# A depthwise convolution shared between DVE and TensorE, in a fused three-layer fp32 kernel

## The reference

```python
def conformer_conv(x, w_pw1, b_pw1, w_dw, b_dw, g, b, w_pw2, b_pw2):
    h = x @ w_pw1 + b_pw1                       # 1024 -> 2048
    a, gate = jnp.split(h, 2, axis=-1)
    h = a * jax.nn.sigmoid(gate)
    h = lax.conv_general_dilated(               # depthwise, causal, 31 taps
        h, w_dw[:, None, :].astype(h.dtype), window_strides=(1,),
        padding=[(CONV_WIDTH - 1, 0)],
        dimension_numbers=("NWC", "WIO", "NWC"),
        feature_group_count=D_MODEL) + b_dw
    h = jax.nn.silu(layer_norm(h, g, b))
    return h @ w_pw2 + b_pw2
```

## Time and profile before

| what | value |
|---|---|
| median of 3 runs | 1508.88 us (1502.25 to 1509.17) |
| the profiled execution | 1508.11 us, span 1506.4 us |
| TensorE busy | 1368.4 us, 91% of the span |
| DVE, ScalarE, GpSimd busy | 373.2, 262.5, 24.3 us |
| chain that ended last | TensorE 88%, DVE 8%, DMA 2% |
| mean granted clock of TensorE | 0.94 |

### The profile page before, as it was taken

One profiled execution on the slowest core, in us unless ns is written; L12 is line 12 of the kernel. 1 busy time (PEld: TensorE's weight loads), 2 busy tenths in 40 slices (PEclk: granted clock), 3 DMA queues, 4 the chain that ended last, 5 costly groups with the idle time before them and its releaser, 6 DMA issues.

```text
span 1506.4 us, 15502 instructions
## 1 busy us (share of the span) xinstructions
PE 1368.4 (91%) x6462; PEld 867.2 (58%) x6462; DVE 373.2 (25%) x831; ACT 262.5 (17%) x549; POOL 24.3 (2%) x48
## 2 busy tenths in 40 slices
PE   7988599999979987699999969988899996999997
PEld 6754434444437754444444448866776685888743
DVE  0013322111131332421211140445403304222201
ACT  1012400101111332210100031231234203000000
POOL 3110000000000000000000000000000000000000
PEclk9999599999999987799999979998999998999998
DMA  9951579999962060569999970411131033544420
GB/s 323 314 167 56 196 302 424 428 427 427 405 243 78 1 223 19 214 263 426 427 425 428 410 263 1 166 58 57 56 112 57 0 112 112 168 137 143 167 84 28
DMA packets 89519, 314.33 MB, mean 209 GB/s; under 512 B 7634, under 2 KB 45014, under 8 KB 75622
## 3 DMA queue, kind: packets, MB, share of 16 engines
q1 hardware_dynamic: 77344, 298.98, 51.4%
q10 hardware_dynamic: 12102, 14.30, 3.3%
HBM read 311.03 MB, written 2.24 MB: 208 GB/s over the span
## 4 chain that ended last, share of the span: by engine, by line
PE 88%; DVE 8%; DMA 2%; issue 1%; ACT 1%; DVEq 0%; ACTq 0%; SPq 0%; POOLq 0%
PE psum L240 39%; PE psum L1347 15%; PE psum L1380 7%; PE psum L578 6%; PE psum L2563 5%; PE psum L1392 4%; PE psum L812 2%; PE psum L459 1%; PE psum L759 1%; PE psum L1522 1%; PE psum L1520 1%; DMA ring<-in_a_w_pw 1%; PE psum L2221 1%; DVE x_nat L531 1%; DVE x_nat L529 1%
## 5 line engine op out<-in xcount | busy, mean ns | idle before, releaser
L240 PE MATMUL psum<-xT,ring 128*128 128x256 f32 (+2 forms) x1792 | 412.6, 392 | 8.8 <-POOLq L439 5.2
L240 PEld LDWEIGHTS psum<-xT,ring 128*128 128x128 f32 x1792 | 345.6, 194 | 72.3 <-issue 15.2
L1347 PE MATMUL psum<-ring,arena 128*64 128x512 f32 x768 | 169.6, 594 | 1.7 <-issue 1.7
L1347 PEld LDWEIGHTS psum<-ring,arena 128*64 128x64 f32 x768 | 54.7, 137 | 104.9 <-issue 104.9
L240 PE MATMUL psum<-arena 128*128 128x128 f32 (+4 forms) x684 | 93.7, 294 | 9.7 <-issue 6.5
L240 PEld LDWEIGHTS psum<-arena 128*128 128x128 f32 (+2 forms) x684 | 85.4, 200 | 14.0 <-issue 10.1
L1380 PE MATMUL psum<-ring,arena 128*64 128x512 f32 x384 | 85.0, 595 | 0.0
L1256 DVE TENSOR_TENSOR arena<-psum,arena 64x512 f32<-64x512 f32 x32 | 34.3, 1071 | 193.4 <-ACT arena L1304 193.4
L2563 PE MATMUL psum<-ring,arena 128*128 128x512 f32 x176 | 75.7, 592 | 0.0
L1304 ACT ACTIVATE arena<-psum 64x512 f32<-64x512 f32 x32 | 18.9, 591 | 262.3 <-PE psum L1347 262.3
L1392 PE MATMUL psum<-arena 128*128 128x512 f32 x128 | 59.2, 605 | 1.8 <-DVE arena L1273 1.8
(11 more groups left out here) (314 smaller groups left out, 1253.6 us busy)
## 6 DMA issues: line engine op xcount, KB each, us to landing
ring<-in_moe_w_gate SPq DMA_DIRECT2D x24, 2048.0 KB, 11.5
ring<-in_moe_w_up SPq DMA_DIRECT2D x24, 2048.0 KB, 15.7
ring<-in_moe_w_down SPq DMA_DIRECT2D x24, 2048.0 KB, 15.9
ring<-in_w_in SPq DMA_DIRECT2D x11, 2048.0 KB, 12.7
ring<-in_w_up SPq DMA_DIRECT2D x22, 1024.0 KB, 7.6
arena<-in_moe_w_gate SPq DMA_DIRECT2D x8, 2048.0 KB, 11.6
ring<-in_w_down SPq DMA_DIRECT2D x5, 2048.0 KB, 7.8
ring<-in_a_w_pw SPq DMA_DIRECT2D x8, 1024.0 KB, 11.3
```

The source lines that it names most:

```text
L240: last = nc.tensor.matmul(dst, lhsT, rhs, start=(n == 0), stop=(n == len(pairs) - 1))
L1347: last = pe.matmul(bank(j)[part, :], tokens[:, k, side * SEATS:side * SEATS + SEATS], weights(u + n, k), start=(k == 0), stop=(k == KC - 1))
```

## The change

Chunks 0 to 3 get their taps on DVE, as 31 steps that multiply a shifted view of the gated chunk by one weight per channel and add it to the accumulator (`taps_here`); the first step adds the bias. Each step waits for the one before (`dve_step`). Chunks 4 to 7 keep the way over DRAM and TensorE. The first projection runs its chunks in the order 0, 4, 1, 2, 5, 3, 6, 7, the weight units are loaded in the order 0, 2, 1, 3, and the statistics take the chunks in the order 0, 4, 1, 2, 5, 3, 6, 7. DVE's steps are cut into pieces, with the gated products of later chunks between them. The tap weights come in two layouts: blocks of four chunks for GpSimd, and four sets of 31 rows for DVE, by twelve small loads and not eight. Buffers move in the arena; the update of `x_nat` with the bias row moves from before the shift to behind chunk 6's centring.

```diff
+ON_PE = 4
+GLU_ORDER = [0, 4, 1, 2, 5, 3, 6, 7]
+GLU_UNITS = [0, 2, 1, 3]
+CENTRED = [0, 4, 1, 2, 5, 3, 6, 7]
+CONV_ORDER = [("glu", 0), ("vec", 0), ("glu", 4), ("glu", 1), ("glu", 2), ("taps", 4), ("glu", 5), ("glu", 3), ("glu", 6),
+              ("taps", 5), ("glu", 7), ("taps", 6), ("taps", 7)]
...
+                for c in range(ON_PE):
+                    sp.dma_start(rows[TAPS * c:TAPS * c + TAPS, 3, :], a["a_w_dw"][0][:, c * P:c * P + P]).then_inc(
+                        consts_loaded, 16)
...
             def shift_sum():
-                pe.wait_ge(conv_out, HALF)
+                pe.wait_ge(consts_made, 2)
+                pe.wait_ge(conv_out, 1)
+                pe.wait_ge(conv_made, HALF - 1)
...
-            for n in range(KC):
-                j = conv_job("glu", n)
+            waiting = None
+            for n, c in enumerate(GLU_ORDER):
+                j = conv_job("glu", c)
                 job_ready(act, j)
...
-                if n >= 5:
-                    taps_out(n - 5)
-                send(n)
-                if n:
-                    fetch_shifted(n - 1)
-            taps_out(HALF - 1)
-            fetch_shifted(KC - 1)
+                if waiting is not None:
+                    fetch_shifted(waiting)
+                    waiting = None
+                if c == 5:
+                    taps_out(4)
+                if c >= ON_PE:
+                    send(c)
+                    waiting = c
+            fetch_shifted(waiting)
...
+            def taps_here(c, first, last):
+
+                for tap in range(first, last):
+                    src, w = glu_of(c)[:, tap:tap + SEQ], tap_scalars[:, TAPS * c + tap:TAPS * c + tap + 1]
+                    if tap == 0:
+                        ins = dve.tensor_scalar(conv[:, c, :], src, w, column("a_b_dw", c), ALU.mult, ALU.add)
+                    else:
+                        ins = dve.scalar_tensor_tensor(conv[:, c, :], src, w, conv[:, c, :], ALU.mult, ALU.add)
+                    dve_step(ins)
+                if last == TAPS:
+                    dve.nop().then_inc(conv_made, 1)
...
-            for n in range(KC):
-                gated(n)
+            gated(0)
+            taps_here(0, 0, 16)
+            gated(4)
+            taps_here(0, 16, TAPS)
+            gated(1)
+            taps_here(1, 0, 15)
+            gated(2)
...
+            gated(3)
+            taps_here(2, 24, TAPS)
+            taps_here(3, 0, 7)
+            gated(6)
+            taps_here(3, 7, 11)
+            dve.wait_ge(shift_summed, 1)
+            dve_step(dve.tensor_scalar(shift_b, psum[:, SHIFT_BANK, 0:SEQ], 1.0 / (HALF * P), None, ALU.mult))
+            for c in CENTRED[:HALF]:
+                dve.tensor_tensor(conv[:, c, :], conv[:, c, :], shift_b, ALU.subtract).then_inc(centred, 1)
+            taps_out(5)
+            taps_here(3, 11, 28)
+            gated(7)
+            taps_here(3, 28, TAPS)
+            dve.tensor_tensor(conv[:, 3, :], conv[:, 3, :], shift_b, ALU.subtract).then_inc(centred, 1)
+            taps_out(6)
             dve.wait_ge(bias_rows_loaded, 16)
```

More of the change, by code:

```diff
@@ L746, in turn_columns @@
                 take_bank(j)
-                pe.wait_ge(consts_loaded, 16 * (sum(len(r) for r in VEC_ROWS) + QUADS))
+                pe.wait_ge(consts_loaded, 16 * (sum(len(r) for r in VEC_ROWS) + QUADS + ON_PE))
                 for tile in range(4):
@@ L752, in taps @@
             def taps(c):
[L753 removed]
+                j, n = conv_job("taps", c), c - ON_PE
                 take_bank(j)
[L755 to L756 removed]
+                pe.wait_ge(shifted_loaded[n], 64)
+                pe.wait_ge(blocks_made, n + 1)
                 for q in range(QUADS):
                     for g in range(CONV_GROUPS):
[L759 to L760 removed]
+                        last = pe.matmul(bank(j)[32 * g:32 * g + 32, 0:SEQ], blocks[:, n % BLOCK_BUFS, q, g, :],
+                                         shifted[:, n, g, 4 * q:4 * q + SEQ], start=(q == 0),
                                          stop=(q == QUADS - 1))
@@ L764, in shift_sum, with mean_part, square_part @@
             def shift_sum():
-                pe.wait_ge(conv_out, HALF)
-                products(psum[:, SHIFT_BANK, 0:SEQ], [(ones[:, :], conv[:, c, :]) for c in range(HALF)]).then_inc(
+                pe.wait_ge(consts_made, 2)
+                pe.wait_ge(conv_out, 1)
+                pe.wait_ge(conv_made, HALF - 1)
+                products(psum[:, SHIFT_BANK, 0:SEQ], [(ones[:, :], conv[:, c, :]) for c in CENTRED[:HALF]]).then_inc(
                     shift_summed, 1)
-            def mean_part(c):
-                pe.wait_ge(centred, c + 1)
-                pe.matmul(psum[:, MEAN_BANK, 0:SEQ], ones[:, :], conv[:, c, :], start=(c == HALF),
-                          stop=(c == KC - 1)).then_inc(mean_summed, 1)
-            def square_part(c):
-                pe.wait_ge(squared, c + 1)
-                last = pe.matmul(psum[:, SQUARE_BANK, 0:SEQ], ones[:, :], squares[:, c % 3, :], start=(c == 0),
-                                 stop=(c == KC - 1))
+            def mean_part(i):
+                pe.wait_ge(centred, i + 1)
+                pe.matmul(psum[:, MEAN_BANK, 0:SEQ], ones[:, :], conv[:, CENTRED[i], :], start=(i == HALF),
+                          stop=(i == KC - 1)).then_inc(mean_summed, 1)
+            def square_part(i):
+                pe.wait_ge(squared, i + 1)
+                last = pe.matmul(psum[:, SQUARE_BANK, 0:SEQ], ones[:, :], squares[:, i % 3, :], start=(i == 0),
+                                 stop=(i == KC - 1))
                 last.then_inc(squares_used, 1)
@@ L786, in _ @@
                     taps(n)
-                    if n == 4:
-                        pe.wait_ge(consts_made, 2)
-                        shift_sum()
-            for c in range(3):
-                square_part(c)
-            taps(6)
-            for c in (3, 4):
-                square_part(c)
-            for c in (4, 5):
-                mean_part(c)
-            square_part(5)
+                if (kind, n) == ("taps", 5):
+                    shift_sum()
+            for i in range(3):
+                square_part(i)
+            taps(6)
+            for i in (3, 4):
+                square_part(i)
+            mean_part(4)
+            for i in (5, 6):
+                mean_part(i)
+                square_part(i)
             taps(7)
-            for c in (6, 7):
-                mean_part(c)
-                square_part(c)
+            mean_part(7)
+            square_part(7)
             j = FJ["pw2"]
@@ L899, in _ @@
             load_norm(0, a["ln_mix_g"][0], a["ln_mix_b"][0])
-            for c in range(KC):
-                squares_of(c)
+            for i in range(KC):
+                squares_of(i)
             act.wait_ge(consts_made, 2)
@@ L947, in _ @@
                 dve_step(dve.scalar_tensor_tensor(x_nat[:, t, :], x_nat[:, t, :], ALPHA, b_pw2, ALU.mult, ALU.add))
-            dve.wait_ge(shift_summed, 1)
-            dve_step(dve.tensor_scalar(shift_b, psum[:, SHIFT_BANK, 0:SEQ], 1.0 / (HALF * P), None, ALU.mult))
-            for c in range(HALF):
-                dve.tensor_tensor(conv[:, c, :], conv[:, c, :], shift_b, ALU.subtract).then_inc(centred, 1)
-            for c in range(HALF, KC):
-                taps_out(c)
+            taps_out(7)
             dve.wait_ge(mean_summed, HALF)
```

102 lines of the change are left out of this document (51 added, 51 removed).

## The result

| what | before | after |
|---|---|---|
| median | 1509.03 us (4 runs, 1502.25 to 1509.2) | 1527.85 us (4 runs, 1526.88 to 1530.06) |
| profiled execution, span | 1508.11, 1506.4 us | 1528.71, 1527.0 us |
| DVE, GpSimd busy | 373.2, 24.3 us | 435.6, 17.1 us |
| second projection starts (in the trace) | 121.49 us | 142.06 us |

The changed kernel is slower: the ratio is 1.0134, with a 95% interval of 1.0113 to 1.0156. The forecast was 1523 in a range of 1514 to 1531. Time and sign came in; a good part of the reason did not, as the experiments show, so that part of the hit is luck.

The account below looks back on a forecast made before the run. The prediction took DVE's column of taps before the last gated product as the bound: 11.4 us, plus 3.5 of DVE's wait and 0.4 of tail, is +15.3 on 1508.1, so 1523, range 1514 to 1531.

Parts of the forecast that it names:

- Every microsecond at the projection passes through: At the second projection's start, 121.49 us before: every microsecond of delay there is a microsecond of the span.
- The steps: DVE's dependent tap steps on 128x256: 484 ns each, 0.524 us from start to start.
- (c): Rival: taps cheaper, 0.36 us a step, TensorE with two gaps the bound; +9, 1517; chance 0.12, shared with a luckier clock.
- (d): Rival: not slower, with the cheap steps and no TensorE gap; -1.2, 1507; chance 0.05.
- This column has no cover: DVE's operations up to the last gated product, 121 taps included, delay it fully: 94.9 us at the earliest against 83.5.
- The reads of chunk 4: Shifted reads before TensorE's taps 4: 8 to 10 us, taps 4 starting at about 49.5, a TensorE gap of 6 us.
- rival (b): Chunk 4's reads fall behind an expert weight, taps 4 start near 57; +22, 1530; chance 0.13.
- The wait at the shift: DVE reaches its wait for TensorE's shift sum at 83.0 and stands 3.5 us, until 86.5; last product at 98.4.
- After the last product: Write, reads and fourteen loads unchanged at 17.4 us, first square at 115.9, then a tail of 20.05 + 0.9 to the projection.
- The sum: Projection at 136.8, +15.3 us: 11.4 from DVE's column, 3.5 from its wait, 0.4 from the tail.

Follow-up runs that it names:

- e1: The changed kernel with thirteen of ScalarE's fourteen loads moved behind its squares and activations, the bias row staying ahead; median 1512.8 us, ratio 1.0053.
- e5: The changed kernel with four expert weight loads on SP's queue held back until taps 4, 5, 5 and 7 are done; median 1512.4 us, ratio 1.0029.
- e6: The changed kernel with the weight loads held as in e5 and every odd tap on DVE left out; median 1508.1 us, ratio 1.0002.
- e4: The changed kernel with every odd tap of the four DVE chunks left out; median 1523.6 us.
- e3: The changed kernel with chunk 7's gated product seven DVE steps earlier, behind step 21 of chunk 3 instead of 28; median 1528.9 us, ratio 1.0148.
- e2: The kernel before with thirteen of ScalarE's fourteen loads moved behind its squares and activations; median 1507.7 us, ratio 1.0006.
- e7: The changed kernel with GpSimd's second block built three times in a row; single execution 1516.6 us.
- e8: The changed kernel, all taps kept, with weights held, loads behind, chunks and products reordered, x update under the second projection; median 1490.9 us, ratio 0.9876.

## Why the prediction was right, and where it was not

**Every microsecond at the projection passes through.** Right for the two profiled executions: 20.6 at the projection, 20.6 at the end. It isn't exact beyond them. The medians lie 18.8 apart, and in e1, e5 and e6 the median fell by 15.1, 15.5 and 19.7 us where the projection moved by 9.2, 10.6 and 15.7; the profiled executions differ by up to 11.6 us in what lies behind the projection, and the equality of 20.6 and 20.6 rests on the two that happen to agree there.

**The steps.** Right in size: 0.52 us between starts, 484 ns each. Rivals (c) and (d), with steps of 0.36 to 0.42 us, are out. The 327 ns that the prediction worked out, as an estimate, from the Trainium skill's page "VectorE: DVE Perf Modes", section "The TRN2 errata", are not what this operation takes in any of these kernels.

**"This column has no cover."** Wrong, and this is the step that failed. Read from DVE's order alone it seemed so, since every step stands ahead of the last product. But in that order stands a wait as well, and all steps ahead of it are covered by what TensorE waits for: leaving out half of the column, on both sides of the wait, gave 1.5 us (e4). Of the seventeen steps behind the wait, seven brought nothing either when they were taken from in front of the product (e3): the last write's landing at 110.8 covers them. Of the 15.3 us forecast, 11.4 were put down to the column; where it is the bound, with the weights held, half of it is worth 5.2 (e5 to e6). And the column itself was put too short: in e5, where it runs without a pause, it ends at 99.1 and not at the 94.9 forecast, and 4.0 us of that are three stands beside GpSimd's builds. That the last product was forecast at 98.4 all the same came from the 3.5 us of waiting put on top. That the time lay in the range is luck as far as this goes: in the kernel as it is, late transfers bind where the sum has the column, and they happened to cost some microseconds more.

**The reads of chunk 4.** Mis-sized: taps 4 were to start at 49.5 and began at 53.94. I took the 9.6 us of the reads at 38.03. That is the median of four reads, and after it is the same (issues from 41.15):

```profile
arena<-glu_scratch ACTq DMA_DIRECT2D x4, 142.0 KB, 9.6
```

But TensorE waits for the last of the four, which with the expert weight in flight came 12.8 us behind the first issue, and 7.9 in e5 without it (40.59 to 48.44). That is rival (b)'s mechanism, with taps 4 between the forecast and its 57, and a projection 20.6 us late, near its 22. The argument against it, half the traffic on ScalarE's queue, missed the point: what counts is what SP's queue has in flight. e5 prices it at 5.5 us at the start of taps 4 and at 9.5, these included, at that of taps 5.

**The wait at the shift.** 3.5 us forecast, 5.45 measured, but that hides two errors. The shift sum ended 6 us late (92.5 against 86.5). Chunk 5's write went out 3.7 us late (67.99 against 64.3), behind the late taps 4, and took 7.6 us and not 9.7, so its reads left 1.6 us late. The last of these then landed 9.6 us behind the first issue, where 6 had been put (85.15 against 80): 3.6 more. Taps 5 at the lower clock added 0.8. DVE came to its wait 4.1 us late too (87.1 against 83.0), 2.6 of it in two operations that stood beside GpSimd's builds (1.48 in the place of 0.41, 2.02 in the place of 0.48), which the sum didn't have; the wait swallowed them. Behind the shift, 11.8 us to the end of the last product are the 11.9 forecast. So all of that product's lateness against the forecast (104.3, 98.4) came through TensorE.

**After the last product.** 17.4 us to ScalarE's being free were 16.1, since this write took 6.5 and not 7.43; the squares at 120.5 (115.9 forecast), then 21.6 to the projection in the place of 20.95, mostly a tap job at the lower clock (5.01 us, 4.27 before). That the two last tap jobs stand behind the fourteen loads was right, and e1 prices it at 7.4 us of issues, 9.2 with what else moved there. The prediction carried these loads as a piece that is the same before and after. It is not: before, e2 says, they were covered.

**The sum.** +15.3 forecast, +20.6 at the projection, +18.8 between the medians. At the projection the 5.3 us between the two are the 5.9 of the last product, 1.3 less to ScalarE's being free, 0.6 more of tail. The chances of the prediction add up to 0.08 for "same" and 0.89 for "slower", where it says 0.09 and 0.88; nothing hangs on it.

## What to carry to other kernels

A long chain in an engine's program bounds the kernel only if the waits inside it are short; before costing its steps, find for each wait what the other side waits for, and leave half of the chain out once to see. Small transfers that a hand-over between engines rests on should not be issued beside megabyte loads on another queue: hold the big ones until the small ones have landed, which here took a wait for each of four loads on SP's queue and gave 10.6 us at the projection. And when a step leaves the critical list, look at what was second: moving thirteen loads gave at most half a microsecond before and 7.4 to 9.2 us after.

## What the runs showed of the hardware

**DVE stands while GpSimd works.** In each of six places that were looked at, a DVE operation on SBUF operands met a build of GpSimd and took 1.48 to 2.08 us, where it takes 0.41 to 0.48: after at 25.88 and 60.1, e7 at 24.93, 26.5 and 28.6, e5 at 79.67. Each ended 0.1 to 0.3 us behind the end of a build. The gated products, which read one operand from PSUM, took 0.48 us at 25.24 as well, in the middle of a build. The Trainium skill states it so: on the page "SBUF — State Buffer", section "Who interferes with whom", a DVE instruction with two SBUF inputs contends with a GpSimd instruction that reads SBUF, and whoever issues second blocks fully. The steps of e7 agree. The first tap at 25.88 has one SBUF input besides its scalars; the section names its operation among those that can use both port pairs, and it stood too.

**Two queues share the DMA engines packet by packet.** From 103 to 105 us after, with the expert weight on SP's queue (q1) and the shifted reads and the write on ScalarE's (q10): packets, MB, share of 16 engines.

```profile
q1 hardware_dynamic: 48, 0.79, 97.1%
q10 hardware_dynamic: 47, 0.05, 8.3%
```

Nearly the same number of packets from either queue, but 16 KB each from one and 1 KB from the other, so ScalarE's queue gets a sixteenth of the bytes. That agrees with the Trainium skill, page "DMA: Bandwidth & Descriptors", section "Queues, rings and completion order", by which an engine goes round the queues with work and takes a packet from each. A transfer of 144 KB in such company took 6.5 us here, 9.6 in e3 and 10.1 before (issued at 66.00), and 1.8 alone (e5).

**The clock after a wait.** Granted clock in two stretches that a tap job fills, the first behind the 9.91 us of TensorE's waiting (after, taps 4), the second without a wait (e5, taps 5); columns as in the earlier trace rows.

```profile
54.00:59.70 5.70, 5.70 (x65) 2.94 (x65) 5.31 (x12) 0.00 (x0) 0.00 (x0) 0.62 0.00 1
```

```profile
75.70:79.20 3.50, 3.50 (x65) 1.92 (x64) 3.14 (x8) 0.47 (x1) 0.00 (x0) 1.00 0.02 5
```

Every tap job that began right behind a wait of 3.85 to 10.19 us took 5.11 to 6.49 us in the place of 3.66 (after, e1, e3 to e7), at a granted clock of 0.55 to 0.71 over the job, so part of it ran at 1.2 of 2.4 GHz. A wait of 4.5 us thus costs over 6. The 1.94 us before taps 7 in e8 were followed by 5.35 as well, behind two earlier waits of 2.47 and 1.10 us; 1.32 us before a tap job in e2, with TensorE busy ahead of it, by 3.66.

**Left open:** the two clusters of e1's times, 10 us apart; only one of its executions was profiled. Such clusters are in other kernels too: of the 39 executions of before beside the experiments, five took 1496.5 to 1502.2 us and all others but the one of 1552 took 1506.7 to 1509.7, and e3 has one at 1515.2 beside four at 1528 to 1530. The cause lies, as far as the profiles go, behind the projection.
